# Five FFN calls of a two-block forward pass on one core: the middle pair of chunks computed by seven block products, down products two chunks behind

## What is computed

```
def swiglu(h, w_gate, w_up, w_down):
    return (jax.nn.silu(h @ w_gate) * (h @ w_up)) @ w_down
...
        x = x + 0.5 * swiglu(rms_norm(x, g[0]), ffn_w_gate[i, 0], ffn_w_up[i, 0], ffn_w_down[i, 0])
...
    gate, up = jnp.split(h @ w_gate_up, 2, axis=-1)
    return x + (jax.nn.silu(gate) * up) @ w_down
```

## Time and profile before

| | us |
|---|---|
| median of three runs | 1307.04 |
| lowest, highest | 1307.03, 1307.15 |
| the profiled execution's own time | 1307.18 |
| its span, from the first to the last instruction | 1305.4 |
| TensorE busy in it | 1289.2 |
| VectorE busy | 846.8 |
| ScalarE busy | 654.5 |
| GpSimd busy | 83.1 |
| data moved by DMA | 256.87 MB |

### The profile page before, as it was taken

The page is one execution under the profiler, slowest core; times in us unless marked ns, Lnnn a source line. Parts: engine busy times, 40 slices in busy tenths (PEclk is TensorE's granted clock), DMA queues, the critical chain, the costliest instruction groups (busy, mean ns, idle before and its releaser), DMA issues.

```text
span 1305.4 us, 17052 instructions
## 1 busy us (share of the span) xinstructions
PE 1289.2 (99%) x6249; PEld 1081.4 (83%) x6249; DVE 846.8 (65%) x929; ACT 654.5 (50%) x769; POOL 83.1 (6%) x195
## 2 busy tenths in 40 slices
PE   9999999999999999999999999999999999999997
PEld 7888889888888887888888877888888987888886
DVE  5665559876555567655556976555567887655554
ACT  6444457445444447544445865444447555544442
POOL 2000004100000002000001300000001300000000
PEclk9999999999999999999999999999999999999999
DMA  9776755446666745666663326666645551676771
GB/s 296 239 231 225 225 194 168 155 136 216 222 225 225 229 173 193 211 225 224 225 225 125 133 97 219 224 225 225 225 177 162 187 175 57 206 226 224 226 227 69
DMA packets 189563, 256.87 MB, mean 197 GB/s; under 512 B 9048, under 2 KB 151022, under 8 KB 189518
## 3 DMA queue, kind: packets, MB, share of 16 engines
q1 hardware_dynamic: 156560, 229.17, 53.3%
q10 hardware_dynamic: 32478, 26.30, 6.4%
q0 software_dynamic: 480, 0.80, 0.4%
HBM read 243.38 MB, written 12.85 MB: 196 GB/s over the span
## 4 chain that ended last, share of the span: by engine, by line
PE 96%; DVE 2%; ACT 1%; issue 0%; POOL 0%; POOLq 0%; DVEq 0%; ACTq 0%
PE ps L275 28%; PE ps L277 28%; PE ps L276 28%; PE ps L372 1%; PE ps L302 1%; PE ps L303 1%; PE ps L304 1%; DVE wl L247 1%; PE ps L1242 1%; PE ps L2972 0%; PE ps L666 0%; PE ps L281 0%; PE ps L2290 0%; PE ps L282 0%; PE ps L285 0%
## 5 line engine op out<-in xcount | busy, mean ns | idle before, releaser
L275 PE MATMUL ps<-wl,hth 128*128 128x512 f32 (+3 forms) x1256 | 490.1, 390 | 1.5 <-DVE htl L2148 0.8
L277 PE MATMUL ps<-wh,htl 128*128 128x512 f32 (+3 forms) x1256 | 485.0, 386 | 0.0
L276 PE MATMUL ps<-wh,hth 128*128 128x512 f32 (+3 forms) x1256 | 484.6, 386 | 0.0
L894 DVE TENSOR_TENSOR wl<-raw,wh 128x2048 fp32r<-128x2048 f32 x120 | 275.1, 2292 | 189.6 <-ACT wh L821 184.4
L821 ACT ACTIVATE wh<-raw 128x2048 fp32r<-128x2048 f32 x120 | 229.5, 1913 | 155.4 <-DMA bounce<-xn 114.8
L275 PEld LDWEIGHTS ps<-wl,hth 128*128 128x128 f32 x1256 | 236.1, 188 | 49.8 <-issue 2.7
L277 PEld LDWEIGHTS ps<-wh,htl 128*128 128x128 f32 x1256 | 236.0, 188 | 47.5
L276 PEld LDWEIGHTS ps<-wh,hth 128*128 128x128 f32 x1256 | 236.2, 188 | 44.8
L247 DVE TENSOR_TENSOR wl<-raw,wh 128x2048 fp32r<-128x2048 f32 (+3 forms) x94 | 207.5, 2216 | 63.1 <-ACT wh L236 62.3
L236 ACT ACTIVATE wh<-raw 128x2048 fp32r<-128x2048 f32 (+3 forms) x94 | 173.5, 1852 | 59.2 <-PE ps L277 43.9
L275 PE MATMUL ps<-wl,prod_h 128*128 128x512 f32 x400 | 156.3, 391 | 0.0
(11 more groups left out here) (423 smaller groups left out, 992.6 us busy)
## 6 DMA issues: line engine op xcount, KB each, us to landing
raw<-in_ffn_w_down SPq DMA_DIRECT2D x88, 512.0 KB, 4.0
raw<-in_ffn_w_gate SPq DMA_DIRECT2D x86, 512.0 KB, 4.1
raw<-in_ffn_w_up SPq DMA_DIRECT2D x86, 512.0 KB, 5.1
raw<-in_w_gate_up SPq DMA_DIRECT2D x44, 512.0 KB, 4.8
raw<-in_even_w_in SPq DMA_DIRECT2D x24, 512.0 KB, 4.5
bounce<-xn ACTq DMA_DIRECT2D x45, 256.0 KB, 3.1
xn<-bounce ACTq DMA_DIRECT2D x45, 256.0 KB, 5.1
raw<-in_w_down SPq DMA_DIRECT2D x22, 512.0 KB, 4.2
```

The source lines that it names most:

```text
L275: nc.tensor.matmul(o, xh, b, start=first, stop=False)
L276: nc.tensor.matmul(o, xh, a, start=False, stop=False)
L277: return nc.tensor.matmul(o, xl, a, start=False, stop=last)
L894: nc.vector.tensor_tensor(wl[:, r, :], raw[:, r, :], wh[:, r, :].bitcast(f32), ALU.subtract)\
```

## The change

Chunks 5 and 6 of each call become a **pair**. Their gate and up are a product of a 2 x 2 block matrix (two token tiles by two feature halves) with another (two feature halves by near chunk 5 and far chunk 6). It is made with seven products of blocks (Strassen's form) instead of eight, each a `quarter` of 12 matmuls. For that:

- Once per call, in chunk 1 and 2, VectorE adds the high and low parts of the features (L1115), scales them by rstd (L1121, with a row that TensorE spreads over the partitions in `spread_rstd`: two multiplications of `ones` with diagonals that VectorE makes), and forms four mixes of blocks (L1127 to L1130). ScalarE makes their high parts, VectorE the low ones (L1134, L1137).
- Per pair VectorE makes four sums of weight blocks: the far sum (L1154) at the end of chunk 3, two near sums (L1161, L1163) and the last sum (L1169, into the ring's slot "sum", which is not loaded) in chunk 4; three of them are split in `arena` (L1178), the last one in the ring. Seven products are added up partly in the banks, partly by five combinations of VectorE after two evictions of ScalarE.
- SP loads the far blocks apart into `arena` in four pieces of 0.5 MB, one behind each of slots 7 to 10. The block b22 is loaded twice, the slot "sum" not at all: one megabyte more per call.
- Down of a chunk comes two chunks later than before in the order. With it come two homes for the products (`prod_h`/`prod_l` and `p_high`/`p_low`), two for the moved blocks, and two bounce buffers. Chunk 0's product is moved like the others; TensorE transposes only the last one.
- The loops over chunks are written out. The slots stand in the order a0 b0 a1 b1 a2 b2 d0 a3 b3 d1 a4 b4 d2 b11 b21 b22 d3 sum a7 b7 d4 a8 b8 d6 a9 b9 d5 a10 b10 d7 d8 d9 d10.

```diff
+        PAIRS = (5,)
+        ORDER, waiting, c = [], [], 0
+        while c < NCH:
+            if c in PAIRS:
+                ORDER += [("b11", c), ("b21", c), ("b22", c), ("d", waiting.pop(0)), ("sum", c)]
+                waiting, c = waiting + [c + 1, c], c + 2
+            else:
+                ORDER += [("a", c), ("b", c)]
+                if len(waiting) > 1:
+                    ORDER.append(("d", waiting.pop(0)))
+                waiting, c = waiting + [c], c + 1
+        LAST_DOWN = [ORDER[-1][1]] + waiting
+        ORDER += [("d", w) for w in waiting]
+        assert len(ORDER) == FFN_SLOTS
+        PLACE = {what: i for i, what in enumerate(ORDER)}
...
+            def load_far(sp, q, c, half, j):
+                if q > 0:
+                    sp.wait_ge(sums_used, 3 * q)
+                at = (SUM1, SUM3)[half]
+                dst, src = gate_up(arena[:, at:at + SLOT].rearrange("p (k n) -> p k n", k=4), half, c * HC + HC)[j]
+                sp.dma_start(dst, src).then_inc(sum_loaded[half], 16)
...
+                for q, g in enumerate(PAIRS):
+                    if 0 <= i - PAIR_LOADS[g] < 4:
+                        sp.wait_ge(weights_used, n + 2)
+                        load_far(sp, len(PAIRS) * f + q, g, *divmod(i - PAIR_LOADS[g], 2))
+        PAIR_LOADS = {g: max(6, PLACE["a", g - 2]) for g in PAIRS}
...
+        def gate_banks(c):
+            if c == 1:
+                return (2, 3)
+            return (1, 2) if c - 2 in PAIRS else (0, 1)
...
+            def plain(c, between=None):
+                if c - 2 in PAIRS:
+                    pe.wait_ge(combined, 5 * (len(PAIRS) * f + PAIRS.index(c - 2)) + 4)
+                elif c > 1:
+                    pe.wait_ge(prod_ready, f * NCH + TURN.index(0 if c == 2 else c - 1) + 1)
...
+            def spread_rstd():
+                pe.wait_ge(mix_diag, f + 1)
+                for tt in range(TT):
+                    m = nc.tensor.matmul(ps[:, 7, tt * P:(tt + 1) * P], ones[:, :], diag[:, tt, :], start=True, stop=True)
+                m.then_inc(mix_row, 1)
...
+            def quarter(b, rows_h, rows_l, w_h, w_l, first, last):
+                for kk in range(4):
+                    w = slice(kk * 512, (kk + 1) * 512)
+                    m = product(bank(b), rows_h(kk), rows_l(kk), w_h[:, w], w_l[:, w], first and kk == 0, last and kk == 3, not first)
+                return m
...
+            def pair(c):
+                q = len(PAIRS) * f + PAIRS.index(c)
+                near = [of_tile(v, 0, 0) for v in (hth, htl)], [of_tile(v, 0, 1) for v in (hth, htl)]
+                pe.wait_ge(prod_ready, f * NCH + TURN.index(c - 1))
+                pe.wait_ge(mix_low, f + 1)
+                pe.wait_ge(sum_low, 3 * q + 1)
+                quarter(3, *of_mix(2), *of_sum(HIGH3, SUM2), True, True).then_inc(sums_used, 1)
+                pe.wait_ge(prod_ready, f * NCH + TURN.index(c - 1) + 1)
+                quarter(0, *near[0], *of_slot("b11", c), True, True).then_inc(weights_used, 1)
+                pe.wait_ge(sum_low, 3 * q + 2)
+                quarter(2, *of_mix(0), *of_sum(HIGH1, SUM1), True, True).then_inc(sums_used, 1)
+                pe.wait_ge(evicted, 2 * q + 1)
+                quarter(0, *near[1], *of_slot("b21", c), False, True).then_inc(weights_used, 1)
+                pe.wait_ge(sum_low, 3 * q + 3)
+                quarter(1, *of_mix(1), *of_sum(HIGH2, SUM3), True, True).then_inc(sums_used, 1)
+                pe.wait_ge(evicted, 2 * q + 2)
+                quarter(2, *of_mix(3), *of_slot("b22", c), False, True).then_inc(weights_used, 1)
+                down(ORDER[PLACE["b22", c] + 1][1])
+                pe.wait_ge(combined, 5 * q + 1)
+                quarter(3, *of_mix(4), *of_slot("sum", c), False, True).then_inc(weights_used, 1)
...
+            def mix_high_parts():
+                act.wait_ge(mix_ready, f + 1)
+                nc.scalar.activation(arena_r[:, MIX_HIGH:MIX_HIGH + 4 * 512], arena[:, MIX:MIX + 4 * 512], ACT.Copy)
+                v = arena_r[:, MIX_HIGH + 4 * 512:MIX_HIGH + 5 * 512].rearrange("p (k t) -> p k t", k=4)
+                nc.scalar.activation(v, rows_turned[:, 4:KT, P:T], ACT.Copy).then_inc(mix_high, 1)
+            def sum_high_of(c, j, high, at):
+                act.wait_ge(sum_ready, 3 * pair_of(c) + j)
+                nc.scalar.activation(arena_r[:, high:high + SLOT], arena[:, at:at + SLOT], ACT.Copy).then_inc(sum_high, 1)
+            def evict(c, j):
+                if j == 0:
+                    act.wait_ge(weights_used, n + PLACE["b11", c] + 1)
+                    nc.scalar.activation(near_1, bank(0), ACT.Copy, scale=rstd[:, 0:1]).then_inc(evicted, 1)
+                else:
+                    act.wait_ge(sums_used, 3 * pair_of(c) + 2)
+                    nc.scalar.activation(far_1, bank(2), ACT.Copy).then_inc(evicted, 1)
...
+                if c in PAIRS:
+                    k = ORDER[PLACE["b22", c] + 1][1]
+                    evict(c, 0)
+                    high(next_of(k))
+                    through("d", k)
+                    evict(c, 1)
+                    through("sum", c)
+                    act_ahead.through(act, n + PLACE["sum", c] + 1)
+                    silu(c + 1)
+                    move_out(c + 1)
+                    silu(c)
+                    act_ahead.through(act, n + PLACE["sum", c] + 2)
+                    move_in(c + 1)
+                    move_out(c)
+                    act_ahead.through(act, n + PLACE["sum", c] + 3)
+                    if early_low(c, k):
+                        high(TURN[TURN.index(c) - 2])
+                    move_in(c)
...
+            def turned_rows():
+                dve_link(dve, nc.vector.tensor_tensor(rows_turned, hth[:, :, :].bitcast(f32), htl[:, :, :].bitcast(f32), ALU.add))
+            def mix_rows():
+                v = rows_turned
+                dve.wait_ge(mix_row, f + 1)
+                nc.vector.tensor_tensor(v, v, repeated(bank(7, T), 1, KT), ALU.mult).then_inc(mix_taken, 1)
+            def mix():
+                v = rows_turned
+                dve.wait_ge(mix_taken, f + 1)
+                a11, a12, a21, a22 = (v[:, 4 * half:4 * half + 4, tt * P:(tt + 1) * P] for tt in range(TT) for half in range(2))
+                nc.vector.tensor_tensor(mixed(2), a11, a21, ALU.subtract)
+                dve_link(dve, nc.vector.tensor_tensor(mixed(0), a21, a22, ALU.subtract))
+                dve_link(dve, nc.vector.tensor_tensor(mixed(1), mixed(0), a11, ALU.subtract))
...
+            def far_sum(c):
+                q = pair_of(c)
+                for loaded in sum_loaded:
+                    dve.wait_ge(loaded, 32 * (q + 1))
+                dve.wait_ge(mix_low, f + 1)
+                nc.vector.tensor_tensor(sum_of(SUM2), sum_of(SUM3), sum_of(SUM1), ALU.add).then_inc(sum_ready, 1)
+            def near_sums(c):
+                q = pair_of(c)
+                w = raw_of("b11", c)
+                dve.wait_ge(sum_ready, 3 * q + 1)
+                nc.vector.tensor_tensor(sum_of(SUM1), sum_of(SUM1), w, ALU.add).then_inc(sum_ready, 1)
+                dve.wait_ge(sum_ready, 3 * q + 2)
+                nc.vector.tensor_tensor(sum_of(SUM3), sum_of(SUM3), sum_of(SUM1), ALU.add).then_inc(sum_ready, 1)
+            def last_sum(c):
+                p = n + PLACE["sum", c]
+                dve.wait_ge(split_ready, p - RING + 1)
+                dve.wait_ge(sum_ready, 3 * pair_of(c) + 3)
+                nc.vector.tensor_tensor(raw[:, p % RING, :], sum_of(SUM3), raw_of("b21", c), ALU.add).then_inc(last_sum_ready, 1)
...
+            def combine(c, j):
+                q = 5 * pair_of(c)
+                if j == 0:
+                    dve.wait_ge(evicted, 2 * pair_of(c) + 2)
+                    m = nc.vector.tensor_tensor(far_1, far_1, bank(3), ALU.subtract)
+                elif j == 1:
+                    dve.wait_ge(sums_used, 3 * pair_of(c) + 3)
+                    m = nc.vector.tensor_tensor(near_1, near_1, bank(1), ALU.add)
+                elif j == 2:
+                    dve.wait_ge(combined, q + 2)
+                    m = nc.vector.tensor_tensor(far_1, far_1, near_1, ALU.subtract)
+                elif j == 3:
+                    dve.wait_ge(weights_used, n + PLACE["b22", c] + 1)
+                    m = nc.vector.tensor_tensor(far_0, bank(2), near_1, ALU.subtract)
+                else:
+                    dve.wait_ge(weights_used, n + PLACE["sum", c] + 1)
+                    m = nc.vector.tensor_tensor(near_1, near_1, bank(3), ALU.add)
+                m.then_inc(combined, 1)
...
+                if c in PAIRS:
+                    k = ORDER[PLACE["b22", c] + 1][1]
+                    low(next_of(k))
+                    through("d", k)
+                    combine(c, 0)
+                    through("sum", c)
+                    combine(c, 1)
+                    combine(c, 2)
+                    combine(c, 3)
+                    dve_ahead.through(dve, n + PLACE["sum", c] + 1)
```

(27 more changed lines are left out.)

394 lines of the change are left out of this document (264 added, 130 removed).

## The result

| | before | after |
|---|---|---|
| median of the runs, us | 1307.10 (1307.03 to 1307.20, 4 runs) | 1316.58 (1315.15 to 1318.18, 4 runs) |
| ratio, 95% interval | | 1.0072 (1.0060 to 1.0084) |
| profiled execution: time, span, us | 1307.18, 1305.4 | 1315.15, 1313.4 |

The account below looks back on a forecast made before the run. TensorE, busy 99% of the span, was taken as the bound. Matmuls saved 13.6 us and stalls gave 5.4 back: 1307.18 - 13.6 + 5.4 = 1298.98, against the median 1298.8 us; range 1293.3 to 1305.0.

Parts of the forecast that it names:

- TensorE's part: Pair's gate and up: 84 matmuls instead of 96, 2.72 us saved per call, 13.6 us in five calls.
- Work added beside it: Extra passes per call, about 32 us on VectorE and 10 on ScalarE, said to fit VectorE's 60 us idle.
- Rival 3: VectorE's two runs and passes after the pair take 0.09 us more per pass: 1310.8 us, slower; chance 0.10.
- the rule that I weighed there: VectorE's pipeline flushes after every operation, so passes would not overlap by 0.09 us; the sum would be rival 3's.
- Run 1: VectorE's work from chunk 1's gate and up to chunk 3: stall 0, by 0.1 us; 0.9 in the first call.
- After the pair: Slots behind the pair: splits come late, stalls of 0.1 to 0.4 us, then 0.3 at the next slot.
- Loads: One megabyte more per call; 6.3 MB in some 30 us, 210 GB/s beside the moves, landing in time: cost 0.
- Run 2: VectorE's sums before and into the pair: 25.1 us, ending at 10.98, wanted by the fifth quarter at 10.88: stall 0.1.
- The first call: Chunk 2's multiplication starts 1.0 us later there, so a stall of 0.9 us before chunk 3.
- The second eviction: In the pair, ScalarE's eviction behind the copy of chunk 4's moved product, ending 13.9, wanted 13.6: stall 0.2 to 0.3.
- Rival 2: Moves become the bound: copies in land in 6.5 us instead of 5.3, 2.8 us a call: 1307.6, no change; chance 0.10.

Follow-up runs that it names:

- e3: Changed kernel with ScalarE issuing the copy in of chunk 5's product after chunk 7's silu: 1310.9 us, ratio 1.0026 to before.
- e5: Changed kernel with SP holding slot 8's load until chunk 0's moved product landed, and slot 12's until chunk 2's: 1309.7 us.
- e1: Changed kernel with each far piece bringing a quarter of its bytes from the second call on, passes keeping their width: 1312.0 us.
- e7: Changed kernel with only slot 12's load held until chunk 2's moved product has landed: 1312.6 us, ratio 1.0044 to before.
- c3: Changed kernel with three orders swapped, loads of slots 8 and 12 held, and chunk 4's low part of the moved product behind the sums': 1300.2 us.
- e6: Changed kernel with only slot 8's load held until chunk 0's moved product has landed: 1316.3 us, ratio 1.0066 to before.

## Why the prediction was wrong

*TensorE's part* held. 12 matmuls fewer a call brought the 13.6 us to well within 1 us, and spreading rstd costs what the transposes cost (0.37 us each).

*Work added beside it* held in size: 138.9 us of VectorE where I had 160, 42.1 of ScalarE where I had 50, each pass 2.25 to 2.29 us with 2.20 to the next. Rival 3 (longer passes) did not happen. The strict reading of the rule that I weighed there (the Trainium skill, VectorE: DVE Perf Modes, Terms) is again not borne out: 371.58 and 373.79 above are the starts of two passes of 2.29 us, 2.21 apart.

*Run 1* was laid right from chunk 1's end on: chunk 3 starts 0.1 us late in calls 2 to 4, as forecast, and 0.6 in the last. *After the pair*, first part: the two slots behind it cost 0.25 and 0.31 us a call, forecast 0.1 to 0.4 and 0.3.

Two steps failed. *Loads: "Cost 0"* is the first. I checked that the far pieces land before they are wanted and that 6.3 MB fit into 30 us. I did not ask **when SP may issue**. SP's release is VectorE's split of the slot three before, and my own run 1 puts the multiplication, the transposition, the adding, the scaling and a low part ahead of its first split: measured, 11.4 us from the end of one split to that of the next. The trace shows a pause there and then a burst: 5 MB issued in 13 us, at a DMA share of 0.95, where I had reckoned with 0.70. (No run took VectorE's work out to see the burst go; that the one makes the other is read from the order, every issue of SP following the end of a split.) The copies of products run beside it on ScalarE's queue, on the same DMA engines. The mean of chunk 2's copy in rose from 4.7 to 6.8 us, with single ones of 8.1; For a copy in I had taken 5.3, and for a copy out 3.6, where chunk 2's took 5.1 to 6.6. By a rule of the Trainium skill (DMA: Bandwidth & Descriptors, Queues, rings and completion order) each DMA engine takes turns between the queues that have work for it, packet by packet. The trace agrees for the second of the two stretches above, where both queues move, 701 packets and 528; by itself the rule doesn't account for the first, where for 3 us only the loads' queue moved. What keeps the copy's first packet back is not shown. That it starts late behind a load just issued is shown: with one at most 1 us ahead of the copy, the median from its issue to its first packet is 3.4 us in after (28 copies) and 3.0 before (39), and with none in the last 4.5 us 1.0 (28 copies of after).

*Run 2: stall 0.1* failed through this. The length is right (25.1 laid; 364.66 to 389.90 is 25.2), its start was 1.46 us late, because in ScalarE's order the rounding of chunk 2's product stands ahead of chunk 3's silu. With a margin of -0.1 us every late start is a stall: 0.8 us a call instead of 0.1.

*After the pair*, second part, is the second: it left out a wait. I had ScalarE's copy out of chunk 5 (0.57 for the issue) and went on to the splits. Between them and chunk 7's silu stands the *issue of the copy in*, which needs the copy out landed: 5.65 us, most of them idle. I counted the copy only for who uses its data, not for who stands behind its issue. This is the largest item, 6.6 of the 21.7 us, and e3 shows it by itself. It is no matter of the burst either: with the loads held (e5) it kept its 6.4 us.

*The first call*: forecast 0.9, measured 4.2. The first copy in takes 7.8 us, the split of the down slot stands behind its rounding, and the clock falls on top. This copy goes out ahead of the pause, beside another bunch: two slots and two far pieces, 3 MB, issued from 30.3 to 36.3.

*The second eviction* (0.2 to 0.3 forecast) cost nothing: the sixth quarter starts at the usual distance in all five calls. In no term of mine were matmuls of the pair and the slots beside it that start 0.230 to 0.236 us apart instead of 0.2267 (1.7 us over the five calls), 0.1 us behind each late start, and small waits before chunks 3 and 4 and the third quarter (some 1.5 us).

**Rival 2** was the right one, with 0.10: late moves, ScalarE in order behind them. Its price of 1307.6 took 6.5 us for the copy in and left out the copy out at chunk 8 (6.6 us) and the first call. I had argued against it with a median of 5.1 us "with the queues as busy": a median of spread loads says nothing of bunched ones. And its cause was only in part the one I gave: with a fourth of the far bytes two other moves were 0.5 to 2.6 us shorter and chunk 2's copy in as late as before (e1); a slot load held back cured that one (e7).

That the plan itself was sound c3 shows: 1300.2 us with the same work, orders and two loads changed, against the forecast of 1298.8. Open stays where 2.6 of e1's 4.5 us come from, what keeps a copy's first packet back behind a load, and whether e5 truly brings more than e6 and e7 together.

## What to carry to other kernels

When work is added to an engine whose progress frees buffers, lay out the loads' issue times as well: here a long run without a release was a pause and then a burst, and the small copies that shared the DMA engines landed late, above all those issued within 1 us of a load. In an in-order queue look at each *waiting* instruction, the issue of a second DMA on a first one's landing above all, and put what the critical engine needs ahead of it; here three such swaps gave 13 us for no work at all. Holding a load back that isn't due yet can be worth more than starting it early: 4 us here.
